# Down projections of a two-layer trunk: W11 ahead of the W22 of the round in front in rounds 1 and 2, and three smaller swaps around Z1 and Z3

## The reference

```
def conv_ffn(h, w_up, conv_w, conv_b, w_down):
    S = h.shape[1]
    u = h @ w_up
    gate, up = u[..., :D_FF], u[..., D_FF:]
    gp = jnp.pad(gate, ((0, 0), (CONV_W - 1, 0), (0, 0)))
    conv = conv_b + conv_w[0] * gp[:, 0:S]
    for i in range(1, CONV_W):
        conv = conv + conv_w[i] * gp[:, i:i + S]
    return (jax.nn.silu(conv) * up) @ w_down

for i in range(DEPTH):
    ...
    x = x + y
    x = x + conv_ffn(rmsnorm(x, ffn_norm[i]), f_w_up[i], f_conv_w[i], f_conv_b[i], f_w_down[i])
return rmsnorm(x, final_norm)
```

## Time and profile before

| | |
|---|---|
| median of three runs | 1082.39 us |
| the profiled execution | 1082.68 us, its span 1080.9 us |
| PE busy | 1071.6 us, 99% |
| VectorE, ScalarE, GpSimd busy | 69%, 46%, 10% |
| chain that ended last | 96% PE: L485 (512-column products) 70%, L545 (down products) 19% |
| mean granted TensorE clock | 1.000 |

### The profile page before, as it was taken

The page is one execution under the profiler, slowest core; times in us unless marked ns, Lnnn a source line. Parts: engine busy times, 40 slices in busy tenths (PEclk is TensorE's granted clock), DMA queues, the critical chain, the costliest instruction groups (busy, mean ns, idle before and its releaser), DMA issues.

```text
span 1080.9 us, 15711 instructions
## 1 busy us (share of the span) xinstructions
PE 1071.6 (99%) x5930; PEld 920.9 (85%) x5930; DVE 751.2 (69%) x1097; ACT 494.3 (46%) x769; POOL 113.4 (10%) x108
## 2 busy tenths in 40 slices
PE   9999999999999999999999999999999999999997
PEld 7888788888899888899888888888888899888897
DVE  6588667676876667789644556867676876667785
ACT  7366554444443334455661345454444433334443
POOL 1100030000100000123021221130000100000122
PEclk9999999999999999999999999999999999999999
DMA  7611032225652225652222211232226652225552
GB/s 228 153 59 60 27 111 98 97 97 184 161 145 98 96 97 170 141 154 91 79 78 98 79 40 59 66 110 98 97 97 184 161 149 97 94 97 170 139 135 91
DMA packets 43804, 121.12 MB, mean 112 GB/s; under 512 B 5250, under 2 KB 10530, under 8 KB 43748
## 3 DMA queue, kind: packets, MB, share of 16 engines
q1 hardware_dynamic: 36020, 106.55, 28.8%
q0 software_dynamic: 4608, 11.54, 6.4%
q10 hardware_dynamic: 3120, 2.28, 1.2%
HBM read 116.93 MB, written 2.88 MB: 111 GB/s over the span
## 4 chain that ended last, share of the span: by engine, by line
PE 96%; DVE 1%; ACT 1%; DMA 1%; issue 0%; SPq 0%; POOL 0%; DVEq 0%; POOLq 0%
PE PS L485 70%; PE PS L545 19%; PE PS L667 1%; PE PS L685 1%; PE PS L849 1%; PE PS L675 1%; DMA X<-xT 1%; PE PS L817 1%; PE PS L851 0%; PE PS L836 0%; PE PS L820 0%; PE PS L746 0%; PE PS L773 0%; PE PS L859 0%; PE PS L786 0%
## 5 line engine op out<-in xcount | busy, mean ns | idle before, releaser
L485 PE MATMUL PS<-XH,WH 128*128 128x512 f32 x992 | 391.3, 394 | 1.0 <-DVE WL L1700 0.6
L485 PE MATMUL PS<-XH,WL 128*128 128x512 f32 x992 | 386.4, 390 | 0.0
L485 PE MATMUL PS<-XL,WH 128*128 128x512 f32 x992 | 386.1, 389 | 0.0
L485 PEld LDWEIGHTS PS<-XH,WH 128*128 128x128 f32 x992 | 186.3, 188 | 41.8 <-issue 2.9
L485 PEld LDWEIGHTS PS<-XL,WH 128*128 128x128 f32 x992 | 186.3, 188 | 38.9 <-issue 1.0
L485 PEld LDWEIGHTS PS<-XH,WL 128*128 128x128 f32 x992 | 186.2, 188 | 39.0
L950 ACT CAST WH<-WRAW 128x1024 fp32r<-128x1024 f32 x134 | 139.5, 1045 | 158.1 <-DMA WRAW<-w_up 107.5
L1389 DVE TENSOR_TENSOR WL<-WRAW,WH 128x1024 fp32r<-128x1024 f32 x134 | 167.4, 1250 | 16.4 <-ACT WH L950 15.8
L1427 DVE TENSOR_TENSOR GS<-PS,R 128x512 f32<-128x512 f32 x44 | 30.4, 692 | 118.2 <-PE PS L485 118.2
L545 PE MATMUL PS<-AH,DH_Z 128*128 128x256 f32 x352 | 97.9, 278 | 0.3
L545 PE MATMUL PS<-AH,DL_Z 128*128 128x256 f32 x352 | 97.4, 277 | 0.0
(11 more groups left out here) (236 smaller groups left out, 1513.0 us busy)
## 6 DMA issues: line engine op xcount, KB each, us to landing
WRAW<-w_up SPq DMA_DIRECT2D x88, 512.0 KB, 3.2
WRAW<-w_bin SPq DMA_DIRECT2D x24, 512.0 KB, 3.2
DRAW_W<-w_down SPq DMA_DIRECT2D x24, 384.0 KB, 3.8
DRAW_W<-w_down SPq DMA_DIRECT2D x24, 320.0 KB, 3.0
WSUM_Z<-w_down SPq DMA_DIRECT2D x12, 384.0 KB, 4.8
WSUM_Z<-w_down POOLq DMA_DIRECT2D x12, 384.0 KB, 6.1
WRAW<-w_qkv SPq DMA_DIRECT2D x8, 512.0 KB, 3.5
WSUM_Z<-w_down SPq DMA_DIRECT2D x12, 320.0 KB, 3.9
```

Of the source, the lines that this page charges most:

```text
L485: last = mm(PS[:, bank], w[:, c:c + P], x[:, kb], start=start and n == 0 and w is wh and x is hi, stop=stop and n == len(kbs) - 1 and w is wl)
```

## The change

TensorE: in rounds 1 and 2 the order Z1, W22 of the round before, W11 becomes Z1, W11, W22 of the round before. SP: the load of W11 for the next round stands ahead of that of W22, since the product that frees its tile ends first. VectorE: `take_w11` stands ahead of the low part of Z3, and `take_w22` behind it; the low part of Z1 for round 2 stands ahead of Z2's sum. ScalarE: the high part of Z1 stands ahead of the second X tile of a round instead of behind it. Round 0 and round 3 keep their orders on TensorE.

```diff
 ROUNDS = ((("Z1", 0), ("W11", 0), ("W12", 0), ("Z2", 0), ("Z4", 0), ("Z3", 0)),
-          (("Z1", 1), ("W22", 0), ("W11", 1), ("W12", 1), ("Z2", 1), ("Z4", 1), ("Z3", 1)),
+          (("Z1", 1), ("W11", 1), ("W22", 0), ("W12", 1), ("Z2", 1), ("Z4", 1), ("Z3", 1)),
...
@@ load_round (SP)
+                if r in (1, 2):
+                    sp.wait_ge(down_done, COUNT[n, "W11"])
+                    load_down(n + 1, "W11")
                 if r:
                     sp.wait_ge(down_done, COUNT[n - 1, "W22"])
                     load_down(n, "W22")
...
                     load_21(n + 2, "Z1")
                     load_21(n + 2, "Z3")
-                if r < 3:
+                if r == 0:
                     sp.wait_ge(down_done, COUNT[n, "W11"])
                     load_down(n + 1, "W11")
+                if r < 3:
                     sp.wait_ge(down_done, COUNT[n, "W12"])
                     load_down(n + 1, "W12")
@@ down_phase (TensorE)
                 for m in (n + 1, n + 2):
                     z1(m)
+                    w11(m)
                     w22(m - 1)
-                    w11(m)
                     w12(m)
@@ down_round (ScalarE)
                 weight_hi(n, "Z3")
+                if r < 3:
+                    weight_hi(n + 1, "Z1")
                 if whole:
                     act.wait_ge(x_taken, COUNT[n - 1, "W22"])
                     x_tile(st, 2 * r - 1)
-                if r < 3:
-                    weight_hi(n + 1, "Z1")
                 weight_hi(n, "W22")
@@ down_rounds (VectorE)
                     weight_lo(m, "Z4")
+                    take_w11(m)
+                    weight_lo(m, "Z3")
                     take_w22(m - 1)
-                    weight_lo(m, "Z3")
-                    take_w11(m)
                     take_w12(m)
                     weight_lo(m, "W22")
                     take_z2(m)
+                    if m == n + 1:
+                        weight_lo(m + 1, "Z1")
                     sum_z2(m + 1)
                     if m == n + 1:
-                        weight_lo(m + 1, "Z1")
                         take_z4(m)
```

## The result

The changed kernel takes 1085.1 us, the median of 13 runs (1083.73 to 1086.41). The kernel before, run beside it, takes 1081.96 us (13 runs, 1080.74 to 1083.1). The ratio is 1.0030 with a 95% interval of 1.0022 to 1.0037: 3.1 us slower, by the interval 2.4 to 4.0. The forecast was 1085.3. The total is right; two of its terms are not, and they nearly cancel.

A forecast was written before the change was run, and what follows sets the result against it. TensorE's nearly unbroken matmuls in the four down stages were taken as the bound. Stage terms 1.25 + 1.05 + 0 + 0.7 = 3.0, taken as +2.9 us on the 1082.39 median, gave 1085.3 us, range 1082.0 to 1088.0.

The forecast's parts named there:

- Price 1: W22's later load delays its low part, Z2's take and so Z3: +1.25 us in the first stage.
- The load took 4.1 us: 309.84: First stage, round 1: W22's load, issued at 305.71, lands at 309.84, so Z3 stalls 0.54 us.
- the prediction's own sign: A first stage of 57.4 us would refute the cost of W22's later load.
- the rival of quick landing: First stage: W22's loads land quicker, so its 1.25 us goes away; +1.7, 1084.1 us; chance 0.17.
- Third stage: Same path behind W22's load, but landing in 3.0 us: no stall, 0.6 us of slack, sum 0.
- Price 2: Five-pair stages: W11 of round 2 waits for its low part, delayed by GpSimd's sum: 0.9 us in each.
- the prediction's list of signs: Pauses expected at Z3 in the first stage and W11 of round 2 in five-pair stages; none at W22, rounds 0 and 1.
- Rest of the five-pair stages: Second and fourth stages, round 2: W22's load late, 0.3 and 0.1 us; W22 waiting for take_z3, 0.2 each.
- Gains: Second and fourth stages: W22 no longer waits for Z3's take; 0.35 and 0.81 us, 1.16 at most.
- Slower spacing "left as it is": Fourth stage: matmul spacing of 0.118 instead of 0.113 us after 1045.16, 0.85 us, stays.
- The rival in which it spreads: First two stages: slower spacing starts early, about 250 matmuls each; +2.3 more, 1087.6 us; chance 0.08.

The follow-up runs named there:

- e3: The changed kernel without its two small swaps (Z1's low part and Z2's sum; Z1's high part and the X tile): 1085.29 us, 1.0030 against the kernel before.
- e5: The changed kernel with W22's load in rounds 1 and 2 of the six-pair stages issued one product later: 1093.62 us, 1.0105 against the kernel before.
- e1: The changed kernel with GpSimd's second sum of squares ahead of the DMA that completes Z1 of round 3: 1082.35 us, 1.0001 against the kernel before.
- e4: The kernel before with the two small swaps (VectorE's and ScalarE's) alone, products in their old order: 1082.36 us, 1.0000 against the kernel before.
- e6: e1 with VectorE's take of Z2 ahead of W22's low part in rounds 1 and 2: 1081.24 us, 0.9990 against the kernel before.
- e8: e7 with VectorE's low part of W11 for round 2 ahead of Z4's sum: 1080.54 us, 0.9981 against the kernel before.
- e9: The changed kernel with W11's low part for round 2 ahead of Z4's take and sum: 1085.06 us, 1.0026 against the kernel before.
- e7: e6 with VectorE's low part of Z1 for round 3 behind the take of Z3: 1080.95 us, 0.9987 against the kernel before.

## Why the prediction was right, and where it was not

- **Direction and mechanism.** The new product order costs (e3), the pauses it removes are worth less than those it makes, and those come through VectorE's strict order. Held.
- **Price 1, first stage: +1.25 us forecast, 0 measured.** The failed step is "The load took 4.1 us: 309.84": it carries a landing time over from one place in SP's queue to another. In the first stage of all eleven profiles the first `load_down` of round 1 (issued at 303 to 304) took 3.8 to 4.8 us, whichever weights it carried: W22 in the old order, W11 in the new; that of round 2 took 4.0 to 4.6. W22's loads, now behind it, took 2.9 to 3.7 in round 1 and 2.9 to 3.4 in round 2. By the prediction's own sign, a first stage of 57.4 us, price 1 is refuted for this execution, and the rival of quick landing, held at 0.17, was the true one for this stage. The path behind the landing was right, as e5 and e1's pause show, and with landings up to 3.7 against the 3.56 at which it begins to cost, the stage has little to spare.
- **Third stage: 0 forecast, 0 measured.** W22's load took 3.0 us there (the issue at 874.45), as assumed.
- **Price 2: 0.9 + 0.9 us forecast, 1.53 (0.75 at Z1, 0.78 at W11) and 1.61 measured.** Its step "a low part beside such a sum took 1.90 us instead of 0.81, a weight sum 1.83; so 1.0 to 1.1 us" took the lengthening of two other overlaps as the price. What the rows have in common is not a lengthening but an end: in the earlier trace rows GpSimd's sum ends at 472.24 + 1.61 = 473.85 and VectorE's operation at 473.51 + 1.04 = 474.55, 0.70 later; in the earlier trace rows 491.25 and 491.93, 0.68 later. With the forecast's own numbers (GpSimd's sum from 473.86, 1.61 us long) the VectorE operation that meets it ends at 476.2: 1.0 us late if that is the sum for Z2, 1.8 if it is Z1's low part. The upper end should have been 1.8 and the value taken at 1.0 or above. The pause at Z1 of round 2 is not in the prediction's list of signs. Measured, the low part ended 1.7 us late in the second stage (2.54 against 0.82) and the sum 1.7 late in the fourth (2.50 against 0.82).
- **Rest of the five-pair stages.** Z3 of round 2: 0.3 and 0.1 forecast, 0.22 and 0 measured. W22 of round 2: 0.2 each forecast, 0.19 and 0 measured. Gains: the pauses of before (0.32 and 0.75) went, as forecast. The second stage lost another 0.14 us to slower spacing.
- **Slower spacing "left as it is".** In the fourth stage this held, 192 matmuls on both sides. The rival in which it spreads did not happen in this profile; e3's second stage and e4's show it.
- **Sum.** Forecast +1.25 + 1.05 + 0 + 0.7; measured 0 + 1.77 + 0 + 0.84. The total came out because an error of +1.25 met one of -0.86, and that is luck. With both at their measured size it would have been +2.6, or about 1085.0. The start of the sum was off too: it stood on 1082.39 us, and the 13 runs have 1081.96; the change itself, by the medians, is +3.1 against the +2.9 forecast.

## What to carry to other kernels

When an operation moves onto another engine's that can hold it up, price the meeting by where the other ends, not by how long some other pair that met took, and ask which of the two goes first. A landing time belongs to a place in the queue as much as to its bytes: before it is carried along with a moved load, look at which load now takes that place, and what cover that one has. And before products are reordered, ask what in the engine behind them starts with a transfer and not with a product, since that part doesn't move: here moving one GpSimd sum (e1) gave back 2.8 of the 3.1 us that the reordering had cost, and only with the moves of e6 to e8 on top was it faster than before. Whether those moves would have done as much in the old product order was not run, so e8's gain is not shown to be the reordering's.

## What the runs showed of the hardware

- **VectorE beside a GpSimd sum.** An operation of VectorE with two SBUF inputs that meets the 128x512 sum of GpSimd and comes second ends 0.68 to 0.70 us after the sum does: changed kernel 475.93 after 475.23 and 1045.55 after 1044.86, e3 476.06 after 475.37, e9 487.08 after 486.40. It looks blocked, not slowed. Where VectorE's operation comes first, it is the sum that takes longer. In the changed kernel's timeline:

```profile
1063.13 0.81 DVE L1498 TENSOR_TENSOR DL_Z<-WSUM_Z,DH_Z 128x640 fp32r<-128x640 f32 x1
...
1063.28 1.82 POOL L1989 TENSOR_TENSOR SS<-SS,SQ 128x512 f32<-128x512 f32 x1 [1.82 <-ACT SQ L984]
```

  Here VectorE's operation keeps its 0.81 us, and the sum takes 1.82 us instead of 1.29 and ends 1.16 us after it. The Trainium skill's "SBUF — State Buffer", section "SBUF: two separate sides", says so: the port pair that the two share is an exclusive lock, and whichever starts first keeps it for the whole instruction. These rows agree with the lock. By the records VectorE's operation started 0.2 us ahead of the sum in the changed kernel (473.39 and 473.62) and still lost. That happened seven times in the eleven profiles, with 0.13 to 0.23 us between the starts, and each time the sum stood straight behind a DMA that GpSimd had issued; in the fourth stage of all eleven VectorE was 0.15 to 0.16 us ahead of a sum with no DMA before it, as in the rows above, and won. GpSimd's spans in a profile are rough, and what the DMA does to the sum's real start is left open.
- **First load of a round.** 3.8 to 4.8 us for 384 KB at the first `load_down` of round 1 of the first stage, 2.9 to 3.7 at the next in the new order; in the third stage, for the same bytes and order, 2.9 and 3.0 in the changed kernel. Why the first stage differs from the third was not found.
- **Two spacings at full clock.** Matmuls of 128x256 run 113.3 or 117.8 ns apart, both at a granted clock of 0.998 to 1.000. Every slow stretch in the eleven profiles begins at a product that starts behind a pause, or whose release came within about 0.2 us of its start (Z3 of round 1 at 473.62 in the changed kernel, released by a take that ended at 473.47, W11 in e6 at 477.64 behind a low part that ended at 477.42, with no pause one can see). It lasts until the stage ends or until a later pause ends it, but not every pause does: in the changed kernel's second stage it goes on over the pause of 0.75 us at Z1 of round 2 and stops at the one of 0.78 at W11. Nor does each pause start one. One stage in it costs up to 1.3 us. e8 against e7 fits the reading that a release well ahead of the product's start keeps it away, but is not proof: e7's second stage was free of it with the same code up to W11 of round 2, where it began in e6. What it is stays open.
